# Gate products between the projection slots of an RG-LRU mixer: another order of eight weight slots, three pairs at a time, four pair buffers

## What is computed

```python
def rglru_mixer(x, w_in, conv_w, conv_b, gate_w, gate_b, a_param, w_out):
    proj = x @ w_in                                   # 1024 -> 2 * 1536
    y_branch, u = jnp.split(proj, 2, axis=-1)
    y_branch = jax.nn.gelu(y_branch, approximate=True)
    u = conv4(u, conv_w) + conv_b                     # causal, 4 taps, per channel
    ub = u.reshape(B, S, LRU_BLOCKS, LRU_BLOCK)       # 6 blocks of 256
    gates = jnp.einsum('bsnk,gnkj->gbsnj', ub, gate_w) + gate_b[:, None, None]
    gates = jax.nn.sigmoid(gates.astype(jnp.float32)).reshape(2, B, S, LRU_WIDTH)
    r, i = gates[0], gates[1]
    log_a = -LRU_C * r * jax.nn.softplus(-a_param.astype(jnp.float32))
    a = jnp.exp(log_a)
    mult = jnp.sqrt(-jnp.expm1(2.0 * log_a))
    b = mult * (i * u.astype(jnp.float32))
    _, h = lax.associative_scan(combine, (a, b), axis=1)    # h_t = a_t h_(t-1) + b_t
    return (h.astype(x.dtype) * y_branch) @ w_out
```

## Time and profile before

| | before |
|---|---|
| median of 3 runs | 2335.21 us |
| lowest and highest | 2331.22, 2339.95 us |
| the execution profiled, its time | 2336.06 us |
| its span in the trace | 2334.3 us |
| granted TensorE clock, mean | 0.963 |
| busy: PE, PEld, DVE, ACT, POOL | 2149.7, 1932.9, 1422.8, 1004.5, 217.2 us |

### The profile page before, as it was taken

The page is one execution under the profiler, slowest core; times in us unless marked ns, Lnnn a source line. Parts: engine busy times, 40 slices in busy tenths (PEclk is TensorE's granted clock), DMA queues, the critical chain, the costliest instruction groups (busy, mean ns, idle before and its releaser), DMA issues.

```text
span 2334.3 us, 37444 instructions
## 1 busy us (share of the span) xinstructions
PE 2149.7 (92%) x14407; PEld 1932.9 (83%) x14407; DVE 1422.8 (61%) x2321; ACT 1004.5 (43%) x1841; POOL 217.2 (9%) x240
## 2 busy tenths in 40 slices
PE   6999899898699999889999789999999999999997
PEld 6876788797498879768888688999999999777775
DVE  5435777678667663054444637997666654666665
ACT  3443434446554344133333334434454444555554
POOL 2101000012200000300000000000223441000000
PEclk9999999998799999969999889999999999999998
DMA  7543567643447853400000323343333335555553
GB/s 254 187 165 117 181 217 237 241 145 135 147 160 252 278 189 103 112 7 1 1 1 37 108 93 129 132 136 120 116 112 118 110 121 171 191 189 191 189 189 135
DMA packets 157431, 333.73 MB, mean 143 GB/s; under 512 B 17382, under 2 KB 69340, under 8 KB 157160
## 3 DMA queue, kind: packets, MB, share of 16 engines
q1 hardware_dynamic: 153896, 321.18, 40.7%
q0 software_dynamic: 3392, 10.52, 1.3%
HBM read 330.58 MB, written 1.08 MB: 142 GB/s over the span
## 4 chain that ended last, share of the span: by engine, by line
PE 74%; DVE 12%; PEld 7%; ACT 2%; issue 2%; SPq 1%; DMA 1%; PEldq 1%; POOL 0%; DVEq 0%; ACTq 0%
PE psum L1975 19%; PE psum L1976 18%; PE psum L1977 18%; PE psum L2491 4%; PE psum L2538 2%; PEld psum L1975 2%; PEld psum L1976 2%; PEld psum L1977 2%; DVE weights_lo L1396 2%; PE psum L2381 2%; PE psum L2387 2%; DVE u_lo L1925 1%; PE psum L2362 1%; PE psum L2267 1%; DVE top_at L1868 1%
## 5 line engine op out<-in xcount | busy, mean ns | idle before, releaser
L1396 DVE TENSOR_TENSOR weights_lo<-weights,weights_hi 128x1024 fp32r<-128x1024 f32 (+2 forms) x336 | 356.5, 1119 | 257.2 <-ACT weights_hi L1012 251.8
L1975 PE MATMUL psum<-input_hi,weights_hi 128*128 128x256 f32 x1288 | 370.0, 287 | 19.1 <-DVE weights_lo L1396 6.7
L1012 ACT ACTIVATE weights_hi<-weights 128x1024 fp32r<-128x1024 f32 (+2 forms) x336 | 290.0, 932 | 194.1 <-PEq L2022 140.1
L1976 PE MATMUL psum<-input_lo,weights_hi 128*128 128x256 f32 x1288 | 366.6, 285 | 0.0
L1977 PE MATMUL psum<-input_hi,weights_lo 128*128 128x256 f32 x1288 | 366.3, 284 | 0.0
L1975 PE MATMUL psum<-input_hi,u_hi 128*128 128x256 f32 x1024 | 300.1, 293 | 0.0
L1977 PE MATMUL psum<-input_hi,u_lo 128*128 128x256 f32 x1024 | 289.7, 283 | 0.0
L1976 PE MATMUL psum<-input_lo,u_hi 128*128 128x256 f32 x1024 | 289.6, 283 | 0.0
L1975 PEld LDWEIGHTS psum<-input_hi,weights_hi 128*128 128x128 f32 x1288 | 249.0, 193 | 34.4 <-issue 31.7
L1925 DVE TENSOR_TENSOR u_lo<-psum,u_hi 128x512 fp32r<-128x512 f32 x256 | 165.0, 686 | 167.4 <-ACT u_hi L1322 166.0
L1976 PEld LDWEIGHTS psum<-input_lo,weights_hi 128*128 128x128 f32 x1288 | 249.2, 193 | 0.0
(11 more groups left out here) (373 smaller groups left out, 4032.8 us busy)
## 6 DMA issues: line engine op xcount, KB each, us to landing
u_rows<-in_peer_u_dram SPq DMA_DIRECT2D x128, 512.0 KB, 3.4
weights<-in_ffn_w_in_dram SPq DMA_DIRECT2D x44, 1024.0 KB, 7.5
v_rows_even<-in_peer_v_dram SPq DMA_DIRECT2D x64, 512.0 KB, 3.5
v_rows_odd<-in_peer_v_dram SPq DMA_DIRECT2D x64, 512.0 KB, 3.4
weights<-in_ret_w_in_dram SPq DMA_DIRECT2D x24, 1024.0 KB, 7.3
ada_rows_in<-in_ada_w_dram SPq DMA_DIRECT2D x24, 1024.0 KB, 5.2
weights<-in_ffn_w_out_dram SPq DMA_DIRECT2D x44, 512.0 KB, 6.5
weights<-in_lru_w_in_dram SPq DMA_DIRECT2D x12, 1024.0 KB, 6.5
```

Source lines behind the costliest of these rows:

```text
L1012: nc.scalar.activation(whi[:, r, at_], wraw[:, r, at_], ACT.Copy).then_inc(s_whi[r], 1)
L1396: ins = nc.vector.tensor_tensor(wlo[:, r, at_], wraw[:, r, at_], whi[:, r, at_].bitcast(F32), ALU.subtract)
L1975: nc.tensor.matmul(o, ah, bh, start=start, stop=False)
L1976: nc.tensor.matmul(o, ah, bl, start=False, stop=False)
```

## The change

The eight slots come in another order, given by a list that all engines follow: the three of u first, then the first gate slot, y0, the second gate slot, y1, y2. The gates are handled three pairs at a time. LR, LI and LA have four buffers each, and LQ is one buffer of scratch: what it held from step to step is now written over LR. LA lies in the idle scratch of the norm (`normed`). The other arrays reach over `ada_bias`, so POOL zeroes that again when it has made the last parts, and the first load of a bias in the second feed-forward network waits for it. The product with the gelu branch is its own step (`gated`), apart from the scan. In the diff come the lists, the memory, then the programs of POOL, ScalarE, VectorE and TensorE.

```diff
+LRU_STEPS = [("u", 0), ("u", 1), ("u", 2), ("gate", 0), ("y", 0), ("gate", 1), ("y", 1), ("y", 2)]
+LRU_UNITS = {"u": 2, "y": 2, "gate": 6}
+LRU_SIZE = {"u": SLOT, "y": SLOT, "gate": 3072}
+LRU_BUFFERS = 4
...
+def lru_unit(kind, n, j):
+
+    at_ = LRU_STEPS.index((kind, n))
+    return UNITS["lru"] + sum(LRU_UNITS[k] for k, _ in LRU_STEPS[:at_]) + j
...
-            LR = sb("lru_r", [P, 2, BANK], F32, st)
-            LI = sb("lru_i", [P, 2, BANK], F32, st)
-            LA = sb("lru_a", [P, 2, BANK], F32, st)
-            LQ = sb("lru_q", [P, 2, BANK], F32, st)
+            LR = sb("lru_r", [P, LRU_BUFFERS, BANK], F32, st)
+            LI = sb("lru_i", [P, LRU_BUFFERS, BANK], F32, st)
+            LQ = sb("lru_q", [P, BANK], F32, st)
...
+        LA = Region("idle scratch", xs_at, 8 * KB).take("lru_a", [P, LRU_BUFFERS, BANK])
...
             for n in range(LB // 2):
                 pool.wait_ge(s_uc, n + 1)
...
+            for n in range(3):
+                gated_input(n)
+            for n in range(2):
+                hidden_parts(n)
+            for n in range(3, 6):
+                gated_input(n)
+            for n in range(2, 6):
+                hidden_parts(n)
+            nc.gpsimd.memset(AB[:, :, :], 0.0).then_inc(s_azero, 1)
...
+            for step_ in (("u", 1), ("u", 2), ("gate", 0), ("y", 0)):
+                split_step(*step_)
+            for n in range(3):
+                sigmoids(n)
+            split_step("gate", 1)
+            decays(range(3))
+            roots(range(3))
+            split_step("y", 1)
+            gelus(0)
+            for n in range(3, 6):
+                sigmoids(n)
+            split_step("y", 2)
+            decays(range(3, 6))
+            split_hi(SLOTS["lru_out"])
+            roots(range(3, 6))
+            gelus(1)
+            gelus(2)
+            split_hi(SLOTS["lru_out"] + 1)
+            split_hi(SLOTS["lru_out"] + 2)
+            split_hi(SLOTS["lru_out"] + 3)
...
+            split_step("u", 1)
+            convolved(0)
+            convolved(1)
+            split_step("u", 2)
+            convolved(2)
+            convolved(3)
+            split_step("gate", 0)
+            convolved(4)
+            split_step("y", 0)
+            convolved(5)
+            split_step("gate", 1)
+            for n in range(3):
+                input_scale(n)
+            for n in range(3):
+                scanned(n)
+            split_step("y", 1)
+            gated(0)
+            gated(1)
+            split_step("y", 2)
+            for n in range(3, 6):
+                input_scale(n)
+            split_lo(SLOTS["lru_out"])
+            for n in range(3, 6):
+                scanned(n)
+            for n in range(2, 6):
+                gated(n)
+            for j in range(1, 4):
+                split_lo(SLOTS["lru_out"] + j)
...
+            for kind, n in LRU_STEPS:
+                r = weights(lru_slot(kind, n))
+                if kind == "gate":
+                    for pair in range(3 * n, 3 * n + 3):
+                        gate_products(pair)
+                else:
+                    for half in range(2):
+                        t_unit(lru_unit(kind, n, half), 0, 0, wview(r), half * 2 * P)
+                used(r)
```

More of the change, by code:

```diff
@@ L775, in _ @@
             ffn("ffn0", 0)
-            for i in range(3):
-                for j in range(2):
-                    wide(SLOTS["lru_in"] + j, W["lru_w_in"], j * LRU_W, i, 2, BANK)
-            for j in range(2):
-                r, use = slot(SLOTS["lru_gate"] + j)
+            for kind, n in LRU_STEPS:
+                if kind != "gate":
+                    wide(lru_slot(kind, n), W["lru_w_in"], n * BANK + (LRU_W if kind == "u" else 0))
+                    continue
+                r, use = slot(lru_slot(kind, n))
                 sp.wait_ge(s_wlo[r], use)
@@ new lines, in split_step, with sigmoids @@
+            def split_step(kind, n):
+                split_hi(lru_slot(kind, n), **lru_size(kind, n))
+            def sigmoids(n):
+                par = n % LRU_BUFFERS
+                if n >= LRU_BUFFERS:
+                    act.wait_ge(s_lh, n - LRU_BUFFERS + 1)
+                for g, dst in enumerate((LR, LI)):
+                    b = take(lru_unit("gate", n // 3, 2 * (n % 3) + g))
+                    for j in range(2):
+                        c = PGB + 12 * g + 2 * n + j
+                        ins = nc.scalar.activation(dst[:, par, half_of(j)], PS[:, b, half_of(j)], ACT.Sigmoid,
+                                                   bias=pcol[:, c:c + 1])
+                    ins.then_inc(s_free[b], 1)
@@ L1164, in _, with roots, gelus @@
+            def roots(three):
+                for n in three:
                     act.wait_ge(s_lq, n + 1)
[L1165 to L1167 removed]
+                    q = LR[:, n % LRU_BUFFERS, :]
+                    nc.scalar.activation(q, q, ACT.Sqrt).then_inc(s_lmult, 1)
+            def gelus(n):
+                for half in range(2):
+                    b = take(lru_unit("y", n, half))
+                    nc.scalar.activation(Y[:, 4 * n + 2 * half:4 * n + 2 * half + 2, :],
+                                         PS[:, b, :].rearrange("p (b t) -> p b t", b=2),
+                                         ACT.Gelu_apprx_tanh).then_inc(s_free[b], 1)
```

185 lines of the change are left out of this document (72 added, 113 removed).

## The result

| | before | changed |
|---|---|---|
| median of 9 runs each, measured side by side | 2337.06 us | 2322.73 us |
| lowest and highest | 2331.22, 2341.69 | 2319.07, 2330.20 |
| ratio (95%) | | 0.994 (0.9925 to 0.9955) |
| the execution profiled, its span | 2336.06, 2334.3 | 2323.82, 2322.0 |
| granted TensorE clock of that execution | 0.963 | 0.966 |

The changed kernel is 14.3 us faster, 0.6%. The forecast was 2327, and its likeliest class was "within 0.5%"; the measured difference is just over that bound, and the interval of the ratio has the bound (0.995) inside it. The time is in the range, 4.3 us under the forecast. The gain in the stage was right to half a microsecond; the rest of the 14.3 us doesn't come from where the prediction looked, and most of the experiments go to that.

What follows compares the result with a forecast made beforehand. TensorE's chain was taken to bound the kernel. Its waits and half-clock losses in the stage were to fall from 37.4 to 28.1 us, a gain of 9.2; 2336.06 less 9.2 gave 2326.9, so 2327, range 2317 to 2334.

Steps and rivals of the forecast that it cites:

- The losses of the stage: TensorE's waits and half-clock losses from LRU projection to output projection: 28.1 us against 37.4 before.
- The gate's split: VectorE's split of the first gate slot, done at 510.6, makes TensorE wait 3.6 us.
- The bank wait: Inside gate 0 TensorE waits 6.1 us for a PSUM bank freed by the sixth convolution's copy, behind y0's split.
- The gelu: In gate 1 TensorE waits 5.6 us for a bank freed by the first gelu, ending at 550.8.
- The second output slot's split: VectorE's split beside three POOL pairs, 10.3 us, done at 598.6; TensorE waits 3.9 us.
- What was costed at nothing: ScalarE's table load before post_norm(2), POOL's new memset and the weight transfers were to add no time.
- The whole lock: Rival: each POOL pair costs a split its full 2.34 us, 2.4 more in all: 2329; chance 0.15.
- Hardly any collision: Rival: POOL's parts hardly delay VectorE's splits, stage ends about 609, time 2314; chance 0.10.
- The clock doesn't fall: Rival: TensorE's half clock after the long waits, 2.8 twice and 1.65 once, isn't paid: 2319.7; chance 0.05.
- The clock doesn't come back: Rival: TensorE stays at 1.2 GHz through y0 and y1 after the bank waits, 20.9 more: 2348; chance 0.05.
- The step that failed: Behind the stage: everything starts earlier and waits for nothing outside it; no term of its own.
- The rule weighed in the prediction: VectorE and POOL share an SBUF port lock; the loser waits out the other's instruction, 2.34 against the row's 1.98.

Runs made afterwards that it cites:

- e1_copy: Changed kernel with VectorE's copy of the sixth convolution moved ahead of y0's split: 2321.99 us, ratio 0.9936.
- e2_gelu: Changed kernel with the first gelu moved ahead of y1's split on ScalarE: 2331.3 us, ratio 0.9974.
- s40: Changed kernel with 40 unread products (4.9 us) in the second step of the feed-forward network behind the stage: 2337.48 us, ratio 1.0003.
- a2_after: Changed kernel run again, unaltered: 2322.52 us, ratio 0.9939.
- e3_out: Changed kernel with VectorE's split of the second output slot moved ahead of scan 5 and gated products 4 and 5: 2319.63 us, ratio 0.9921.
- e4_all: Changed kernel with the sixth convolution's copy, the second output slot's split and the first gelu all moved earlier: 2311.84 us, ratio 0.9893.
- e5_warm: Changed kernel with 44 and 32 unread products in the bank waits of gate 0 and gate 1: 2328.54 us, ratio 0.9964.
- e7_two: Changed kernel with the sixth convolution's copy and the second output slot's split moved earlier, the gelu unmoved: 2323.78 us, ratio 0.9947.
- s16: Changed kernel with 16 unread products (1.9 us) in the second step of the feed-forward network behind the stage: 2334.29 us, ratio 0.9988.
- bs40: Kernel before with 40 unread products (4.9 us) in the second step of the second feed-forward network: 2343.8 us, ratio 1.0029.

## Why the prediction was right, and where it wasn't

- **The losses of the stage.** Predicted 28.1 us of waits and half clock, 37.4 before. (The 37.4 stand, 24.8 and 12.6; the shorter waits of before are three, not four.) Measured: waits 4.56, 6.27, 4.93 and 3.38, which is 19.1, and 17.9 us at half clock, which loses 8.9: 28.1 (19.14 and 8.95). Even the parts of the half clock sum to the 8.9 predicted, but by luck: 2.9, 4.4, 4.8 and 5.7 us, where I had 3.3, 5.6, 5.6 and 3.3. The stage ended at 621.4, predicted 622.3.
- **The gate's split.** It was done at 510.6 as predicted; the wait was 4.6 instead of 3.6 since the stage began 0.57 earlier and VectorE's two convolutions took half a microsecond more (4.96, and 5.88 beside POOL, for which I had 4.8 and 5.5).
- **The bank wait.** Predicted 6.1, ended by a copy at 522.7; measured 6.27, copy at 521.98 to 522.7. (The second profile of the changed kernel has 4.96: there the half clock ahead of it lasted 3.0 us longer, which made the wait 1.3 shorter.) e1_copy removed it by moving that copy alone: the cause is shown.
- **The gelu.** Predicted a wait of 5.6, measured 4.93: the gelu ended at 549.6 instead of 550.8, the chain to it having begun earlier. What stood behind the roots was y1's split and a table load, as the prediction said; e2_gelu shows that changing their order moves the wait and doesn't remove it.
- **The second output slot's split.** This is the mis-sized term: 10.3 us predicted, 8.4 measured. I let three of POOL's pairs fall on it. The first began at 584.4 and fell on the four gated products before the split, which took 4.57 instead of 2.9; the next ones grow to 3.7 and 4.2, so two fell on the split. The sum of both is 13.0 against my 13.2, so that the error cancelled, and the wait was 3.4 for 3.9.
- **What was costed at nothing.** The table load ahead of post_norm(2) took 1.28 at 617.06, four microseconds before the second squares; the memset ran from 599.6 to 601.4 with the first bias load issued at 621.4. No transfer entered.
- **Rivals.** The whole lock falls: three splits beside one pair took 6.62, 5.52 (three quarters of a slot) and 6.58, +2.0 each, not +2.34. Hardly any collision falls by the same rows. "The clock doesn't fall" is wrong for this kernel; its 2319.7 also left out one of the sum's two terms of 1.65, with which it would have been 2318.0. "The clock doesn't come back" is wrong in the stage: it was granted 1.00 from 529.6 to 541.5 (y0) and from 558 to 570 (y1).
- **The step that failed** is the last sentence of the path, "What is after the stage starts earlier and waits for nothing outside it", and with it the sum against one profiled execution. It is true that nothing there waits for anything new. But the mixing stage took 271 to 284 us, and the piece before it 385.3 to 390.8 where nothing was put into it, with the clock granted. By the profiles, behind the stage the changed kernel gave back 5.3 us ahead of the mixing (a granted clock of 0.94 against 0.96) and won 7.1 in it; with 0.2 behind it and 0.6 before the stage the two spans differ by 12.3. The last 2.0 of the 14.3 lie between the medians and the profiled executions, in no trace. So the 4.7 us beyond the stage are located in part only. In the profiles the rest of the program moved by 5 us down and 7 us up from before's, which was worth a term of its own: with it my chance of faster by over 0.5% (11.7 us) would have been larger than 0.28.

The rule weighed in the prediction (the Trainium skill, "SBUF — State Buffer", Who interferes with whom: the loser waits out the other's whole instruction) is near as a bound. The rows show 2.0 per pair at the splits that met one, under the 2.34 that the pair takes alone, and 1.9 where POOL works back to back. The other side, which the prediction left out of its last term, goes the same way: POOL's pair grows from 2.34 to 3.3 and to 4.2, by 0.9 and 1.9, and two pieces of a split take 2.3.

## What to carry to other kernels

Ask of a reordering which single instruction frees the next bank or buffer, and what stands ahead of it on its engine: a copy of 0.7 us behind a split made TensorE wait 6.3 us here (moving it won 3.2 in the stage, and 2.4 more by the clock), and putting copies and the split of the next wanted slot ahead of work that nobody waits for won as much again in the stage as the whole change (151.0 to 141.5). Compare kernels stage by stage in their traces before comparing medians: half a percent of this kernel's time is decided by the clock of a stage that wasn't touched. And compare once more with a few microseconds of unread work put in, in both kernels: here that left 5 to 6 of the 14.3 us, with 8.6 and 11.0 us in the stage.

## What I had not expected of the hardware

- The length of a wait doesn't say what the clock does behind it. The same wait of 4.56 us ahead of gate 0, with the same work around it, was followed by 2.8 to 2.9 us at half clock in the changed kernel, e1_copy and s40, and by 5.6 to 6.2 us in a2_after, e2_gelu, e3_out, e4_all, e5_warm, e7_two and s16. A wait of 3.60 (e1_copy) was followed by none, one of 3.38 (changed) by 5.7. The longer half clock behind gate 0's wait cost next to nothing, since the bank wait behind it ended by VectorE's copy at the same time and was 1.3 us shorter for it:

```profile
522.13 0.58 PE L2060 MATMUL psum<-lru_hi,weights_hi 128*128 128x256 f32 x1 [4.96 <-DVEq L1668]
```

That is a2_after, 52.4 us into the stage; the changed kernel has its 6.27 at the same 52.4.
- The first projection slot, behind the same 1.7 us of idle time, took 12.0 us in the two profiles of the changed kernel and 13.3 in e2_gelu, e4_all, e5_warm and s16, whose edits all lie behind it (13.6 in bs40).
- Unchanged code of 1700 us took 1697.4 to 1709.5 us in the profiles of kernels that differ only ahead of it. The mixing stage carries most of that, 271.2 us at a granted clock of 0.99 to 283.9 at 0.93, and its first 28.8 us tell the short ones (0.94 and 0.99) from the long (0.61 to 0.67).
